# Seven block products for eight in the second feed-forward layer of a hybrid decoder block

## What is computed

```
h = modulate(rms_norm(x, g_ffn2), sh3, sc3)
x = x + 0.5 * gt3 * ((silu(h @ w1_b) * (h @ w3_b)) @ w2_b)      # w1_b, w3_b: 1024 x 2816, w2_b: 2816 x 1024
return rms_norm(x, g_final)
```

## Time and profile before

| | us |
|---|---|
| median of 3 runs | 2393.91 |
| lowest and highest | 2393.04, 2394.76 |
| span of the profiled execution, first to last instruction | 2389.7 |
| PE busy in it | 2308.2 |
| POOL busy | 1100.9 |
| DVE busy | 909.8 |
| ACT busy | 320.6 |

### The profile page before, as it was taken

How to read it: one execution, slowest core, us unless ns; L and a number is a source line. 1 busy time by engine, 2 the same in 40 slices (tenths; PEclk the granted TensorE clock), 3 DMA queues, 4 the chain that set the end, 5 groups by cost and what they waited for, 6 DMA issues and landing times.

```text
span 2389.7 us, 27721 instructions
## 1 busy us (share of the span) xinstructions
PE 2308.2 (97%) x10370; PEld 1898.9 (79%) x10370; DVE 909.8 (38%) x1219; ACT 320.6 (13%) x372; POOL 1100.9 (46%) x824
## 2 busy tenths in 40 slices
PE   5899999999999899999999989999999999999997
PEld 4788788878888678888888867887888888888886
DVE  6645124331012699475665544436011101110134
ACT  3311000000011331010101121115110001000112
POOL 3354444444445453444444455543544444444452
PEclk8999999999999999999999999999999999999998
DMA  7344124321121332223222144411111111111111
GB/s 282 106 147 133 44 85 117 114 79 47 50 47 50 115 97 75 84 80 88 84 75 88 53 167 132 137 47 36 53 49 48 48 49 47 50 46 51 41 39 70
DMA packets 258446, 194.29 MB, mean 81 GB/s; under 512 B 21524, under 2 KB 238752, under 8 KB 257248
## 3 DMA queue, kind: packets, MB, share of 16 engines
q1 hardware_dynamic: 234752, 154.52, 21.3%
q10 hardware_dynamic: 23648, 39.20, 5.2%
HBM read 167.34 MB, written 25.17 MB: 81 GB/s over the span
## 4 chain that ended last, share of the span: by engine, by line
PE 93%; DVE 3%; ACT 1%; SPq 1%; issue 0%; DMA 0%; POOL 0%; DVEq 0%; POOLq 0%; ACTq 0%
PE unit_a L486 32%; PE unit_b L486 31%; PE unit_c L486 12%; PE unit_d L486 12%; PE unit_d L726 1%; PE unit_a L565 1%; SPq L340 1%; PE unit_b L565 1%; DVE xr L1105 1%; PE unit_c L609 1%; DVE rstd L1062 1%; PE unit_c L711 1%; PE unit_d L701 1%; PE unit_d L724 1%; PE unit_c L522 0%
## 5 line engine op out<-in xcount | busy, mean ns | idle before, releaser
L456 POOL TENSOR_TENSOR w_high<-raw,ones 128x512 fp32r<-128x512 f32 x408 | 545.3, 1336 | 1220.1 <-PE unit_b L486 395.7
L458 POOL TENSOR_TENSOR w_low<-raw,w_high 128x512 fp32r<-128x512 f32 x408 | 555.8, 1362 | 32.0
L486 PE MATMUL unit_a<-h_high,w_high 128*128 128x512 f32 x1072 | 333.7, 393 | 6.0 <-POOL w_low L458 4.7
L486 PE MATMUL unit_a<-h_low,w_high 128*128 128x512 f32 x1072 | 331.2, 390 | 0.0
L486 PE MATMUL unit_a<-h_high,w_low 128*128 128x512 f32 x1072 | 331.0, 390 | 0.0
L486 PE MATMUL unit_b<-h_high,w_high 128*128 128x512 f32 x1072 | 330.5, 389 | 0.0
L486 PE MATMUL unit_b<-h_high,w_low 128*128 128x512 f32 x1072 | 330.1, 389 | 0.0
L486 PE MATMUL unit_b<-h_low,w_high 128*128 128x512 f32 x1072 | 330.0, 389 | 0.0
L1153 DVE TENSOR_TENSOR s<-s,unit_b 128x1024 f32<-128x1024 f32 x44 | 53.7, 1221 | 655.5 <-PE unit_b L486 652.9
L486 PEld LDWEIGHTS unit_a<-h_high,w_high 128*128 128x128 f32 x1072 | 200.6, 189 | 48.4 <-POOL w_low L458 5.1
L486 PEld LDWEIGHTS unit_a<-h_low,w_high 128*128 128x128 f32 x1072 | 202.0, 188 | 42.5
(11 more groups left out here) (233 smaller groups left out, 2266.0 us busy)
## 6 DMA issues: line engine op xcount, KB each, us to landing
raw<-in_w_a SPq DMA_DIRECT2D x60, 512.0 KB, 4.1
raw<-in_w_b SPq DMA_DIRECT2D x60, 512.0 KB, 3.8
raw<-in_w_in SPq DMA_DIRECT2D x44, 512.0 KB, 3.9
ada_raw<-in_w_ada SPq DMA_DIRECT2D x8, 2048.0 KB, 7.9
ada_raw<-in_w_ada SPq DMA_DIRECT2D x8, 1536.0 KB, 7.0
ada_first<-in_w_ada SPq DMA_DIRECT2D x8, 1024.0 KB, 14.2
sg_kept<-s ACTq DMA_DIRECT2D x16, 512.0 KB, 2.6
s<-sg_kept ACTq DMA_DIRECT2D x16, 512.0 KB, 3.3
```

The source lines that it names most:

```text
L456: pool.tensor_tensor(high, raw[:, r, rows, :], one, ALU.mult).then_inc(high_split, 1)
L458: pool.tensor_tensor(w_low[:, r % 2, rows, :], raw[:, r, rows, :], high.bitcast(F32), ALU.subtract).then_inc(slab_split, 1)
L486: last = pe.matmul(unit[u][:, t], w, x[:, k, t], start=(k == 0 and part == 0), stop=(k == kts - 1 and part == 2))
```

## The change

The second feed-forward layer is computed with seven block products where a product of 2 x 2 blocks has eight (Winograd's form of Strassen's scheme). Two neighbouring column tiles of w1 (or w3) are one matrix of 1024 x 256, cut into four blocks a11, a12 (rows 0 to 511 and 512 to 1023 of the first tile) and a21, a22 (of the second), each 4 k tiles of 128 columns. h is cut into b11, b21, b12, b22, each 512 channels by 512 positions. A block product is 4 k tiles x 3 parts = 12 matmuls of 512 columns into one bank.

- Of the 22 column tiles two are done whole as before (`whole_tiles`: four slabs); the other 20 in 5 chunks of two pairs. One `matrix` is a pair of w1 or of w3; a chunk is four matrices and one `down` with 4 k tiles (24 matmuls a tile, 8 tiles). After the first matrix of chunk 1 comes `first_down`, w2 with the two whole tiles as k tiles. The first chunk and the last are written out, chunks 2 to 4 are a loop.
- Sums of h blocks (t1 to t4): once, by DVE (`act_sums`, four operations of 2048 columns), with high parts by ACT (`sum_high`) and low parts by DVE (`sum_low`), right behind the norm.
- Sums of weight blocks: POOL, four operations of 128x512 a matrix. The high parts of the seven weight operands go from POOL to ACT (`weight_high`), the low parts stay on POOL. For the whole tiles and w2 POOL makes both.
- The split weights are a ring of four operands of 4 k tiles each (`operand`) instead of two slots of 8; an operand may be overwritten when the product four places before is done.
- The products go into four banks: units A, B for w1, C, D for w3. The first product's bank is copied out by ACT (`first_copy`), DVE adds up the others (`out_of`), and three products are added in PSUM to banks that PE wrote before, once DVE has read them.
- A w1 matrix takes 5 DVE operations of 512 columns; a w3 matrix 5, and 4 gated products and 4 low parts of g. Products and low parts work from SBUF alone except one product that reads PSUM.
- Each matrix of a pair is loaded in one transfer of 1 MB, rows of 1 KB, into two neighbouring raw slots (`load_matrix`); the blocks are then strided views of it (`raw_blocks`). w2 comes in four transfers of 512 KB a chunk.
- The norm before the layer writes into the new places of h and takes the k tiles of the second half of the positions in the order 0, 4, 1, 5, 2, 6, 3, 7.

The core of the diff:

```
-    ffn("ffn2", False)
+    out.append(("ffn2", 0, (1, 1, 1 + 6 * 4, 1 + 6 * 4), 0, 0))
+PRODUCTS = (("a11", "b11", 0, True), ("s2", "t2", 1, True), ("s1", "t1", 2, True), ("s3", "t3", 3, True),
+            ("a12", "b21", 0, False), ("s4", "b22", 2, False), ("a22", "t4", 3, False))
...
+        def raw_blocks(slots):
+            both = pair_slab(slots[0])
+            return {"a11": both[:, 0:HK, 0, :], "a12": both[:, HK:KD, 0, :],
+                    "a21": both[:, 0:HK, 1, :], "a22": both[:, HK:KD, 1, :]}
...
+            def load_matrix(here, n):                                     # SP
+                v = (v1_pairs, v3_pairs)[n % 2]
+                sp.wait_ge(operand_low, here.raw_free[n][1])
+                r = here.slots[n][0]
+                sp.dma_start(pair_slab(r).rearrange("p k e n -> p k (e n)"),
+                             v[:, :, here.f1 + n // 2, :]).then_inc(matrix_loaded[n % 2], 16)
...
+            def matrix(here, n):                                          # POOL
...
+                mixed = w_mixed[:, :, :]
+                summed(a_["a21"], a_["a11"], a_["a21"], ALU.subtract, 1)
+                summed(mixed, a_["a22"], a_["a21"], ALU.subtract, 2)
+                low(0)
+                summed(a_["a11"], mixed, a_["a11"], ALU.add, 3)
+                low(1)
+                summed(mixed, a_["a12"], mixed, ALU.subtract, 4)
+                for q in range(2, N7):
+                    low(q)
+            def down(here):                                               # POOL
+                for n in range(8):
...
+                    pool.wait_ge(operand_used, here.down_op + n - 3)
+                    whole(*operand(n % 4), here.high0 + n, two_tiles(r)[:, n % 2, :, :], one)
...
+            def matrix(here, n):                                          # PE
...
+                banks_free(here, n)
+                for q, (_, b_name, to, anew) in enumerate(PRODUCTS):
+                    pe.wait_ge(operand_low, o + q + 1)
...
+                    if not anew and to == 0:
+                        pe.wait_ge(first_copied, here.matrix[n] + 1)
+                    elif not anew:
+                        pe.wait_ge(evacuated, done + to)
+                    wh, wl = operand((RING[n] + q) % 4)
+                    bh, bl = act_operand[b_name]
+                    for k in range(HK):
+                        for part, (w_, x) in enumerate(((wh, bh), (wh, bl), (wl, bh))):
+                            last = pe.matmul(bank(w, to), w_[:, k, :], x[:, k, :],
+                                             start=(anew and k == 0 and part == 0),
+                                             stop=(k == HK - 1 and part == 2), skip_group_check=True)
+                    last.then_inc(operand_used, 1)
...
+            def tile_down(here, m):                                       # PE
...
+                wh, wl = operand(m % 4)
+                for k in range(4):
+                    pe.wait_ge(fg_ready, 2 + 4 * here.pair[k // 2] + 3 + k % 2)
...
+            def weight_high(here, n, q):                                  # ACT
...
+                act.wait_ge(operand_used, here.op[n] + q - 3)
+                act.activation(operand((RING[n] + q) % 4)[0], weight_plain(PRODUCTS[q][0], slots),
+                               ACT.Copy).then_inc(operand_high, 1)
...
+                dve.wait_ge(first_copied, here.matrix[n] + 1)             # DVE, matrix
+                out_of(1, 2, u2, u2, bank(w, 1))
+                out_of(2, 3, to[1, 1], u2, bank(w, 2), 1)
+                out_of(3, 4, to[1, 1], to[1, 1], bank(w, 3), 2)
+                if w:
+                    gated_block(4, 3, 1, 1, 1, to[1, 1])
+                    dve.wait_ge(operand_used, o + 5)
+                    gated_block(5, 0, 2, 0, 0, bank(w, 0))
+                    low_block(1, 1, 1)
+                    out_of(6, 6, to[0, 1], u2, bank(w, 2), 1)
+                    gated_block(7, 6, 3, 0, 1, to[0, 1])
+                    low_block(2, 0, 0)
+                    out_of(8, 7, to[1, 0], u2, bank(w, 3), 1)
+                    gated_block(9, 8, 4, 1, 0, to[1, 0])
+                    low_block(3, 0, 1)
+                    low_block(4, 1, 0)
+                else:
+                    out_of(4, 6, to[0, 1], u2, bank(w, 2), 1)
+                    out_of(5, 7, to[1, 0], u2, bank(w, 3), 1)
```

More of the change, by code:

```diff
@@ L461, in _, with whole @@
             split(0, True)
-            with pool.Fori(1, at["end"].slab // 4) as i:
+            with pool.Fori(1, at["ffn2"].slab // 4) as i:
                 split(i, False)
+            two_by_two = ones[:, :].rearrange("p (a b n) -> p a b n", a=1, b=1).to_broadcast([P, 2, 2, P])
+            def whole(high, low, n, plain, by):
+                pool.tensor_tensor(high, plain, by, ALU.mult).then_inc(whole_high, 1)
+                pool.wait_ge(whole_high, n + 1)
+                pool.tensor_tensor(low, plain, high.bitcast(F32), ALU.subtract).then_inc(operand_low, 1)
@@ L466, in _ @@
+            for n in range(1, 4):
+                matrix(here, n)
+            down(here)
+            with pool.Fori(2, PAIRED + 1) as c:
+                here = Chunk(c)
+                for n in range(4):
+                    matrix(here, n)
+                down(here)
         @block.tensor
@@ L1009, in _, with silu, whole_silu @@
             norm(2, at["norm2"].h)
-            for n in range(3):
-                up("ffn2", n)
-            here, ends = at["ffn2.down2"], at["end"]
+            def silu(tile, unit_or_bank):
+                return act.activation(tile, unit_or_bank, ACT.Silu)
+            def whole_silu(e):
+                act.wait_ge(operand_used, (2, 6)[e])
+                silu(fg_two[:, 2 + e, :], unit[2 * e][:, :]).then_inc(silu_done, 1)
+                act.wait_ge(silu_done, e + 1)
+                act.sem_inc(unit_free[2 * e], 1)
@@ new lines, in _ @@
+            for which in range(4):
+                pair_silu(here, 0, which)
+            matrix(here, 1, after=False)
+            for n in (2, 3):
+                matrix(here, n)
+            for which in range(4):
+                pair_high(here, 3, which)
+            with act.Fori(2, PAIRED + 1) as c:
+                here = Chunk(c)
+                for n in range(4):
+                    matrix(here, n)
+                for which in range(4):
+                    pair_high(here, 3, which)
@@ L1013, in _ @@
+            ends = at["end"]
             with act.Fori(0, KD // 2) as i:
@@ new lines, in first_down @@
+            def first_down(g):
+                for m in range(KD):
+                    if m % 2 == 0:
+                        dve.wait_ge(first_tile_used, m // 2 + 1)
+                    else:
+                        dve.wait_ge(operand_used, 15 + m // 2 + 1)
+                    dve.scalar_tensor_tensor(out=x_res[:, m, :], in0=unit[C_ + m % 2][:, :], scalar=column(g, m),
+                                             in1=x_res[:, m, :], op0=mul, op1=add).then_inc(unit_free[C_ + m % 2], 1)
@@ new lines, in _ @@
+            act_sums()
+            sum_low("t2", 1)
+            sum_low("t1", 2)
+            sum_low("t3", 3)
+            whole_product(0)
+            sum_low("t4", 4)
+            whole_product(1)
+            whole_low(0)
+            whole_low(1)
+            here = Chunk(1)
+            matrix(here, 0)
+            first_down(gate[1][:, :])
+            for n in range(1, 4):
+                matrix(here, n)
+            down(None, gate[1][:, :], used=operand_used, first=here.down_op)
+            with dve.Fori(2, PAIRED) as c:
+                here = Chunk(c)
+                for n in range(4):
+                    matrix(here, n)
+                down(None, gate[1][:, :], used=operand_used, first=here.down_op)
@@ L1498, in _ @@
+            here = Chunk(PAIRED)
+            for n in range(4):
+                matrix(here, n)
+            clear_sums(3)
+            down(None, gate[1][:, :], 3, used=operand_used, first=here.down_op)
             dve.wait_ge(root_done, 7)
```

405 lines of the change are left out of this document (364 added, 41 removed).

## The result

The changed kernel takes 2367.2 us (median of four runs, 2366.68 to 2368.67), the kernel before beside it on the same chip 2393.5. The ratio is 0.989 with a 95% interval of 0.9876 to 0.9904: 26.3 us less, where the prediction said 28.1 less and forecast 2365.8. The profiled execution of the changed kernel took 2368.67 us, its span is 2366.9.

A forecast was written before the change was run, and what follows sets the result against it. PE bounds the kernel: -54.4 (matmuls) + 6.2 (start) + 1.6 (its clock) + 1.5 (bank wait) + 5 x (2.4 + 1.0) (seams) = -28.1 us, giving 2365.8; own range 2352 to 2376, 8 in 10 for 2345 to 2380.

The forecast's parts named there:

- cost the clock: After a wait PE runs at the lower clock for a while: 1.0 us at each of five seams, 1.6 at the start.
- seam waits: Between each chunk's fourth matrix and first w2 tile, PE waits 2.4 us for DVE's low block, five times.

The follow-up runs named there:

- e6: Against the changed kernel, eleven of the twelve matmuls of each matrix's sixth product left out, so the output is not the whole sum; 2325.85 us.
- e3: Against the changed kernel, second half of the layer's first w1 product in natural block order and the first operand buffer released after its fourth block; 2362.98 us.
- e5: Against the changed kernel, each pair of weight slabs loaded again by two transfers of 512 KB, seven products kept; 2367.82 us.
- e12: Against the changed kernel, ACT instead of POOL makes the high parts of the last four whole w1 operands at the start of the layer; 2364.77 us.
- e4: Against the changed kernel, PE asks for bank D in the second matrix only at its third product; 2363.19 us.
- e8: Against the changed kernel, DVE's activation sums and their low parts each made as four instructions of 512 columns instead of one of 2048; 2369.81 us.
- e1: Against the changed kernel, ACT makes the high parts of the sixteen whole w2 operands of each chunk, POOL only the low parts; 2355.30 us.
- e10: Against the changed kernel, POOL takes over three of the seven high parts of each matrix from ACT; 2360.86 us.
- e11: Against the changed kernel, POOL takes over five of the seven high parts of each matrix from ACT; 2400.60 us.

## What to carry to other kernels

When PE is the bound, a removed matmul is worth its pitch, but it also uncovers the places where PE is fed by a short chain through other engines: count there, in microseconds, who stands on the port that DVE and POOL share, and make the engine with time to spare wait (one semaphore wait gave 17 us). Instructions that exclude each other take turns one by one, so to cut one side's instructions into pieces gives the port to the other side; only fewer operations, or a third engine with its own way, relieve a port that is full. A product next to such a place is cover and gives less than its pitch (e6: 41.4 us of 49.9).

## What the runs showed of the hardware that I had not expected

- The same wait does not always cost the clock. Behind seam waits of 2.13 to 2.17 us PE dropped to the lower of its levels (1.2 of 2.4 GHz) in three cases of five in the changed kernel, e3, e5 and e12, and in two of five in e4 and e8. It is no plain lottery either: in all six profiles a seam that lost the clock and one that kept it alternate from the second seam on. What sets which comes first no run shows. Two such windows of the changed kernel, of equal waits:

```profile
2051.60:2055.60 4.00, 3.96 (x17) 3.30 (x18) 1.35 (x2) 0.00 (x0) 0.86 (x1) 1.00 0.78 251
2173.80:2177.80 4.00, 4.00 (x11) 3.14 (x12) 0.50 (x1) 0.00 (x0) 0.00 (x0) 0.57 0.79 256
```

  Behind waits of 0.52 to 0.98 us (e1, five cases) and 1.37 to 1.47 (e10, four) it never did; behind 1.98 to 2.07 (e11) it did once of five, behind 3.35 to 3.39 (e6) four times of five. In the changed kernel a drop costs 1.6 us more than the same wait without one (1.9 for 0.3). An expected cost is therefore a mean, and one profile can be off it by one or two such drops.
- POOL's back-to-back pitch for a 128x512 operation whose operands wait on one another is 1.37 us for a duration of 1.29.
- Before any change of the code acts, the profiles of the fourteen kernels with the same first 1600 us differ by 3 us (1600.49 to 1603.45), so a step of 2 us is read from a place behind which the code differs, not from two spans.
